# A two-block transformer kernel on one core: the joint before the second block's first site, with rows transposed before the final norm scales them

## The chip, the cores and the metric

One Trainium2 chip, one core of it. The time is the device time of one execution in microseconds, the median of three runs for the kernel before. TensorE does the matrix products, VectorE and ScalarE the elementwise work, GpSimd a few adds and some loads, SyncE issues the weight loads.

## The reference

The input is one sequence of 256 tokens with 1024 features. A first block of two layers (attention, convolution, Fourier and spatial gating branches, modulated by a conditioning vector) ends in a root-mean-square norm. A second block follows, two layers of three parts each, which the kernel calls sites 0 to 5: feed-forward, mixer, feed-forward, twice.

```
x, xc = layer 0, layer 1                      # first block
x = rmsnorm(x, final_g)                       # the final norm
for layer in range(2):                        # second block
    x = x + 0.5 * rmsnorm(swiglu(rmsnorm(x, g[0])), g[1])   # site 0 or 3
    x = x +       rmsnorm(mixer(rmsnorm(x, g[2])), g[3])    # site 1 or 4
    x = x + 0.5 * rmsnorm(swiglu(rmsnorm(x, g[4])), g[5])   # site 2 or 5
rmsnorm(x, g) = x * rsqrt(mean(x * x) + 1e-6) * g
```

All of it is float32. The products of the second block split each operand into a high part, rounded to the fast float32r format, and a low part, the remainder, and add three products: high by high, low by high, high by low.

## The kernel before

**Residual.** `X` holds the 256 tokens as two tiles t of 128 rows, each handled in two halves hf of 512 columns. At the end of layer 1 four output banks, one for each (t, hf), are multiplied by a gate row on VectorE (`out_scaled`, L1133, into two buffers `ytmp`, one for each hf) and added to `X`, by GpSimd (L619), or by VectorE for the pairs in `ADDED` (L1137). `x_half(L, t, hf)` names whichever add it is.

**The joint.** ScalarE takes the squares of `X` and the root of the final norm (L891 to L896), VectorE the reciprocal (L1368) and `final_scaled` (L1372), which multiplies `X` by it and by the gain `final_g`. TensorE then transposes `X` in chunks of 128 columns (`turned`, L2215) into banks, ahead of it `warm` filler products (L2206) that nobody reads. ScalarE makes the high part of chunk c out of the bank (`input_high`, L912), with the gain of site 0's norm as scale, VectorE the low part HL (`input_ready`, L1394). The root of site 0's own norm is not applied to the inputs: it is taken meanwhile (`x_square`, `inverse`), laid out as a row by two small products (`norm_sum`, L2232) and a copy (`norm_row`, L921), and multiplied into the gate sums behind the products (`gate_scaled`, L1446).

**A feed-forward site.** Hidden columns come in 22 chunks of 128. Units of 1024 columns of weights, numbered a, a+1, ... from `unit_base[i]`, go through a ring of three slots in SBUF (1 MB a slot, two units), each split by `high` on ScalarE (L879) and `low` on VectorE (L1361, its semaphore `s_low` counts the units) into six buffers. Units a to a+4 are gate, up, gate, up and down of the first pair; a+5 gate and a+6 up of the next pair, a+7 the second down row of the first. TensorE's order is gate_up(0), norm_sum, gate_up(1), down(0), and then a loop of gate_up(0), down(1), gate_up(1), down(0) per pair; L2254 and L2255 are the products of gate and up, L1765 those of down. VectorE sums the halves of a bank (`gate_parts` L1442, `up_parts` L1454), multiplies by the silu of the gate (L1459) and makes `hidden_low` (L1468); ScalarE does `silu` (L946) and `hidden_high` (L952). ScalarE's order in the first pair is silu(0), high(a+6), hidden_high(0), high(a+7). VectorE's is low(a+4), gate_scaled, low(a+5), multiplied, hidden_low(0), low(a+6).

**Queues.** Each engine works its own list in the order written. SyncE issues a weight load into a slot when the last low of the slot's two units is done (L498, in the loop L527): the gate slot of the second pair waits for low(a+2), the up slot for low(a+3), the down slot for low(a+7). In the joint VectorE does the lows of units 0 to 3 ahead of `out_scaled`. GpSimd issues the load of the gain row of site 0's second norm when `final_scaled(1, 1)` is done, and behind it that of `alibi`, a table of the mixer (L557).

## Time and profile before

| | |
|---|---|
| runs | 1490.28, 1492.75, 1494.66 us |
| median | 1492.75 us |
| profiled execution, its own time | 1492.96 us |
| its span, first to last instruction | 1491.2 us |
| busy in it | TensorE 1452.5 us (97%), VectorE 985.8 (66%), ScalarE 702.3 (47%), GpSimd 66.2 (4%) |
| mean granted TensorE clock | 0.996 |
| HBM traffic | 162 GB/s over the span |

The runs lie within 0.3% of each other. The time of the profiled execution is its span and 1.8 us around it. Times in the rows of a trace are microseconds from the start of the span. A busy share says how full an engine is, not where it stands still.

### The profile page before, as it was taken

What the parts mean: (1) busy time and instruction counts of PE and PEld (TensorE: products, weight loads), DVE (VectorE), ACT (ScalarE), POOL (GpSimd) and SP (SyncE); (2) the same over time, 40 slices, a digit from 0 to 9 for tenths busy, and PEclk for the clock granted to TensorE, in tenths of its full rate; (3) what the DMA queues carried; (4) which work ended last, traced back from release to release, by engine and by line L of the source; (5) the groups of instructions that cost most, each with busy time, mean ns of one, the idle gap of its engine ahead of it and who ended that gap; (6) DMA issues with size and microseconds to landing.
All of it is one profiled execution on the core that took longest, in us unless ns stands there. A gap on an engine that the chain in (4) does not pass through costs nothing.

```text
span 1491.2 us, 22138 instructions
## 1 busy us (share of the span) xinstructions
PE 1452.5 (97%) x8141; PEld 1174.5 (79%) x8141; DVE 985.8 (66%) x1631; ACT 702.3 (47%) x1212; POOL 66.2 (4%) x91
## 2 busy tenths in 40 slices
PE   5999999999999999999999999999999999999998
PEld 3778746877855888889888888878888888788887
DVE  2588335165345777777787777786777776877776
ACT  3433136141245444466566444464444756554444
POOL 0200120020101000000010000000000001000000
PEclk9999999999999999999999999999999999999999
DMA  9532166245316556646434566546566554455662
GB/s 331 196 91 79 57 194 219 85 132 170 112 57 208 170 178 205 208 156 170 142 114 156 169 198 200 193 159 193 169 197 199 178 145 143 127 167 171 195 197 88
DMA packets 197717, 242.96 MB, mean 163 GB/s; under 512 B 4464, under 2 KB 179088, under 8 KB 197520
## 3 DMA queue, kind: packets, MB, share of 16 engines
q1 hardware_dynamic: 194560, 229.43, 48.5%
q0 software_dynamic: 2512, 10.49, 2.0%
q10 hardware_dynamic: 576, 2.10, 0.4%
q8 instruction: 46, 0.75, 0.2%
q14 instruction: 23, 0.19, 0.0%
HBM read 240.95 MB, written 1.05 MB: 162 GB/s over the span
## 4 chain that ended last, share of the span: by engine, by line
PE 89%; DVE 4%; DMA 3%; ACT 2%; issue 1%; SPq 0%; POOL 0%; DVEq 0%; ACTq 0%; POOLq 0%
PE bank L1765 39%; PE bank L2254 20%; PE bank L2255 10%; PE bank L1884 5%; PE bank L2162 1%; PE bank L1743 1%; DMA weight_ring<-in_w_ada 1%; DVE input_split L1394 1%; DMA weight_ring<-in_w_ffn_up 1%; DVE weights_low L1361 1%; PE bank L2107 1%; PE bank L2070 1%; PE bank L2029 1%; ACT weights_high L879 1%; PE bank L2079 1%
## 5 line engine op out<-in xcount | busy, mean ns | idle before, releaser
L1361 DVE TENSOR_TENSOR weights_low<-weight_ring,weights_high 128x1024 fp32r<-128x1024 f32 x328 | 393.1, 1221 | 133.4 <-ACT weights_high L879 133.2
L2254 PE MATMUL bank<-input_split,weights_high 128*128 128x512 f32 x1344 | 479.2, 399 | 1.6 <-DVE input_split L1394 1.3
L879 ACT ACTIVATE weights_high<-weight_ring 128x1024 fp32r<-128x1024 f32 x328 | 334.9, 1048 | 105.3 <-PE bank L1765 62.0
L2255 PE MATMUL bank<-input_split,weights_low 128*128 128x256 f32 x1344 | 376.9, 280 | 0.0
L2254 PEld LDWEIGHTS bank<-input_split,weights_high 128*128 128x128 f32 x1344 | 252.4, 188 | 65.6 <-issue 2.2
L2255 PEld LDWEIGHTS bank<-input_split,weights_low 128*128 128x128 f32 x1344 | 253.7, 189 | 3.0
L1765 PE MATMUL bank<-weights_high,hidden_high 128*128 128x512 f32 x352 | 138.0, 392 | 0.3 <-DVE hidden_low L1468 0.3
L1765 PE MATMUL bank<-weights_low,hidden_high 128*128 128x512 f32 x352 | 137.9, 392 | 0.0
L1765 PE MATMUL bank<-weights_high,hidden_low 128*128 128x512 f32 x352 | 137.0, 389 | 0.0
L946 ACT ACTIVATE silu_gate<-gate_sum 128x256 f32<-128x256 f32 x88 | 36.8, 418 | 206.8 <-DVE gate_sum L1446 203.8
L1765 PE MATMUL bank<-input_split,weights_high 128*128 128x256 f32 x640 | 117.9, 286 | 1.4 <-DVE input_split L1394 1.3
L1765 PEld LDWEIGHTS bank<-input_split,weights_high 128*128 128x128 f32 x640 | 99.3, 191 | 3.5 <-issue 1.4
L952 ACT ACTIVATE hidden_high<-hidden 128x256 fp32r<-128x256 f32 x88 | 36.8, 418 | 128.2 <-DVE hidden L1459 126.7
L1765 PE MATMUL bank<-weights_high,input_split 128*128 128x256 f32 (+1 forms) x384 | 90.2, 323 | 0.5 <-issue 0.5
L1765 PE MATMUL bank<-input_split,weights_low 128*128 128x256 f32 x320 | 90.4, 283 | 0.0
L1765 PEld LDWEIGHTS bank<-weights_high,hidden_high 128*128 128x128 f32 x352 | 66.1, 188 | 15.7 <-issue 0.6
L1765 PEld LDWEIGHTS bank<-weights_high,hidden_low 128*128 128x128 f32 x352 | 66.1, 188 | 14.5
L1765 PEld LDWEIGHTS bank<-weights_low,hidden_high 128*128 128x128 f32 x352 | 66.1, 188 | 10.8
L1884 PE MATMUL bank<-hT,weight_ring 128*128 128x256 f32 (+1 forms) x304 | 73.5, 399 | 0.5 <-ACT hT L701 0.5
L1765 PEld LDWEIGHTS bank<-weights_high,input_split 128*128 128x128 f32 x384 | 64.4, 190 | 8.6 <-issue 3.5
L1884 PEld LDWEIGHTS bank<-hT,weight_ring 128*128 128x128 f32 x304 | 58.3, 194 | 13.3 <-issue 5.7
L1468 DVE TENSOR_TENSOR hidden_low<-hidden,hidden_high 128x256 fp32r<-128x256 f32 x88 | 37.4, 425 | 45.2 <-ACT hidden_high L952 45.2
(329 smaller groups left out, 2098.9 us busy)
## 6 DMA issues: line engine op xcount, KB each, us to landing
weight_ring<-in_w_ffn_gate SPq DMA_DIRECT2D x44, 1024.0 KB, 5.3
weight_ring<-in_w_ffn_up SPq DMA_DIRECT2D x44, 1024.0 KB, 5.3
weight_ring<-in_w_ffn_down SPq DMA_DIRECT2D x44, 1024.0 KB, 4.9
weight_ring<-in_w_in SPq DMA_DIRECT2D x32, 1024.0 KB, 5.3
weight_ring<-in_w_ada SPq DMA_DIRECT2D x24, 1024.0 KB, 6.8
weight_ring<-in_w_out SPq DMA_DIRECT2D x16, 1024.0 KB, 5.0
weight_ring<-in_w_in SPq DMA_DIRECT2D x24, 512.0 KB, 4.9
gain_row<-in_norm_gains POOLq DMA_DIRECT2D x6, 512.0 KB, 4.0
```

What stands on the lines that cost most here:

```text
L879: A(unit_in(WH, U), unit_source(U), ACT.Copy).then_inc(s_high, 1)
L946: A(sgate[:, par, :], gsum[:, par, :], ACT.Silu).then_inc(s_silu, 1)
L952: A(HBH[:, par if to is None else to, :], hbuf[:, par, :], ACT.Copy).then_inc(s_hh, 1)
L1361: TTn(unit_in(WL, U), unit_source(U), unit_in(WH, U).bitcast(F32), ALU.subtract).then_inc(s_low, 1)
L1394: STT(HL[:, c, :], B[X_BANK[c]][:, half * T:(half + 1) * T], vT[:, 2, R_PRE + 8 * i + c:R_PRE + 8 * i + c + 1], HH[:, c, :].bitcast(F32), ...
L1468: TTn(HBL[:, to, :], hbuf[:, par, :], HBH[:, to, :].bitcast(F32), ALU.subtract).then_inc(s_hl, 1)
L1743: last = mm(b[32 * (k % 4):32 * (k % 4) + 32, q * T:(q + 1) * T], CS[:, k, :], cols(n)[:, k, :], start=(k < 4), stop=(k >= 4), skip_group_ ...
L1765: last = mm(o, lhs(x), rhs(y), start=start and m == 0, stop=stop and m == 2, skip_group_check=True)
L1884: last = mm(b[out_rows, 0:ncol], lhs(k), hT[:, k, 0:ncol], start=(k == 0), stop=(k == KD - 1))
L2029: last = mm(b[:, sg * T:(sg + 1) * T], FA[:, 2 * sg + tl, m, cs * P:(cs + 1) * P], dft_n[:, cs, tl, :], start=(g == 0), stop=(g == 3))
L2254: mm(b[:, :].rearrange("p (h n) -> p h n", h=2), unit_in(WH, U)[:, k, :], HX[:, k, :, :], start=(k == 0), stop=False, skip_group_check=True)
L2255: last = mm(b[:, 0:T], unit_in(WL, U)[:, k, :], HH[:, k, :], start=False, stop=(k == KD - 1), skip_group_check=True)
```

## The change

The edits, all of them about the joint and site 0:

- `ADDED` for layer 1: VectorE adds (0, 1) too, so that GpSimd has two adds and VectorE two.
- VectorE does the lows of units 0 and 1 alone ahead of `out_scaled`; low(2) comes after the HLs of site 0, low(3) after `final_scaled(1)`.
- TensorE transposes `X` as it leaves layer 1, unscaled. `input_high` and HL multiply by `first_gain`, the product of final_g and site 0's gain, made at the start from a row added to the packed vectors.
- `final_scaled(t)` still scales `X` in place, as the residual needs it, but tile 0 after its transposes (`x_read`) and before the HLs, tile 1 after the HLs and low(2).
- The final root of tile 0 is taken as before; the last square and the root of tile 1, and the squares of site 0's norm, come after the eight input_high on ScalarE.
- `inverse(0)` also multiplies by the final norm's inverse root, and eps times the mean by the final root's square, in small operations on 128x2.
- For site 0 `norm_sum` moves from between gate_up(0) and gate_up(1) to the middle of gate_up(1), `gate_parts` behind `inverse`, and high(4) ahead of the root.
- Filler: one `warm` instead of six ahead of site 0's transposes, and one more between the tiles.
- GpSimd's two loads wait for `s_low` of 31 as well.

```diff
-ADDED = [{(0, 1), (1, 1)}, {(1, 1)}]
+ADDED = [{(0, 1), (1, 1)}, {(0, 1), (1, 1)}]
...
             pool.wait_ge(*at("final_scaled", 1, 1))
+            pool.wait_ge(s_low, unit_base[0] + 31)
             load(gain_row[:, :], I["norm_gains_2"][0, 1].partition_broadcast(P), "gain_loaded")
...
+            final_square(0, 0)
+            final_square(0, 1)
+            final_root(0)
+            final_square(1, 0)
...
             def site_norm(i):
-                for hf in range(2):
-                    x_square(i, 0, hf)
+                if i == 0:
+                    act.wait_ge(*at("first_gain"))
+                else:
+                    for hf in range(2):
+                        x_square(i, 0, hf)
...
+                if i == 0:
+                    final_square(1, 1)
+                    final_root(1)
+                    for hf in range(2):
+                        x_square(0, 0, hf)
                 for hf in range(2):
                     x_square(i, 1, hf)
+                if i == 0:
+                    high(unit_base[i] + 4)
...
+            TTn(first_gain[:, :], vT[:, 2, R_PRE:R_PRE + 8], vT[:, 2, R_FG:R_FG + 8], ALU.mult).then_inc(*done("first_gain"))
...
                 if L:
-                    for unit in range(EARLY):
+                    for unit in range(2):
                         low(unit)
...
+            def final_scaled(t):
                 dve.wait_ge(*at("final_root", t))
-                dve.reciprocal(stat[:, 12 + t:13 + t], stat[:, 8 + t:9 + t]).then_inc(*done("inverse", "final", t))
+                dve.reciprocal(stat[:, 56 + t:57 + t], stat[:, 54 + t:55 + t]).then_inc(*done("inverse", "final", t))
                 dve.wait_ge(*at("inverse", "final", t))
+                dve.wait_ge(*(at("x_T", "site", 0, 5) if t else at("x_read", 0)))
...
+            final_scaled(0)
...
+                if i == 0:
+                    low(2)
+                    final_scaled(1)
+                    low(3)
...
+                if i == 0:
+                    TTn(stat[:, 12:14], stat[:, 12:14], stat[:, 56:58], ALU.mult).then_inc(*done("inverse", "both"))
+                    dve.wait_ge(*at("inverse", "both"))
...
-                gate_parts(0, a + 1)
+                if i:
+                    gate_parts(0, a + 1)
                 inverse(i)
+                if i == 0:
+                    gate_parts(0, a + 1)
...
-                        pe.wait_ge(*(at("x_new", i - 1, t, c // 4) if i else at("final_scaled", t, c // 4)))
+                        pe.wait_ge(*(at("x_new", i - 1, t, c // 4) if i else x_half(1, t, c // 4)))
...
-                warm(1 if i else WARM)
+                warm(1)
                 turned(0, (0, 1, 2, 3))
                 warm(1)
                 turned(0, (4, 5, 6, 7))
+                if i == 0:
+                    warm(1)
                 turned(1, (0, 1, 2, 3, 4, 6, 5, 7))
...
                     for q in range(2):
+                        if between is not None and q:
+                            norm_sum(between)
...
-                norm_sum(i)
+                if i:
+                    norm_sum(i)
...
-                gate_up(1, a + 2, f0 if n else None)
+                gate_up(1, a + 2, f0 if n else None, between=None if i else 0)
```

## Rows read from the trace of the kernel before

**Rows 1.** The page, part 4: the chain that ended last, share by engine.

```profile
PE 89%; DVE 4%; DMA 3%; ACT 2%; issue 1%; SPq 0%; POOL 0%; DVEq 0%; ACTq 0%; POOLq 0%
```

**Rows 2.** Chain of waits in the joint: start, length, what.

```profile
476.02 2.06 DVE input_split L1394 x5
```

**Rows 3.** Timeline of TensorE: start, length, line, operation, tiles, shape, count, idle before.

```profile
459.99 7.10 PE L2162 MATMUL bank<-weight_ring,gated 128*128 128x512 f32 x16 [0.57 <-DVE gated L1309]
...
473.39 0.68 PE L2215 MATMUL bank<-const_base,residual 128*128 128x128 f32 x4 [1.15 <-DVE residual L1372]
...
488.83 0.39 PE L1765 MATMUL bank<-weights_high,hidden_high 128*128 128x512 f32 x1
...
513.99 0.40 PE L1765 MATMUL bank<-weights_high,hidden_high 128*128 128x512 f32 x1
...
581.08 0.40 PE L1765 MATMUL bank<-weights_high,hidden_high 128*128 128x512 f32 x1
```

**Rows 4.** Timeline of VectorE, the joint and site 0's loop.

```profile
463.86 3.50 DVE L1361 TENSOR_TENSOR weights_low<-weight_ring,weights_high 128x1024 fp32r<-128x1024 f32 x3 [2.09 <-ACT weights_high L879]
467.28 1.28 DVE L1133 TENSOR_TENSOR scaled_out<-bank,gate_rows 128x512 f32<-128x512 f32 x2
...
471.46 0.93 DVE L1137 TENSOR_TENSOR residual<-residual,scaled_out 128x512 f32<-128x512 f32 x1
...
474.09 1.41 DVE L1372 SCALAR_TENSOR_TENSOR residual<-residual,stat,gain_row 128x512 f32<-128x512 f32 x2
...
478.67 0.88 DVE L1394 SCALAR_TENSOR_TENSOR input_split<-bank,vectors_T,input_split 128x256 fp32r<-128x256 f32 x2 [0.21 <-ACT input_split L912]
...
512.36 0.43 DVE L1468 TENSOR_TENSOR hidden_low<-hidden,hidden_high 128x256 fp32r<-128x256 f32 x1 [0.48 <-ACT hidden_high L952]
...
553.95 2.36 DVE L1361 TENSOR_TENSOR weights_low<-weight_ring,weights_high 128x1024 fp32r<-128x1024 f32 x2 [0.53 <-ACT weights_high L879]
...
578.11 0.43 DVE L1468 TENSOR_TENSOR hidden_low<-hidden,hidden_high 128x256 fp32r<-128x256 f32 x1 [0.48 <-ACT hidden_high L952]
```

**Rows 5.** Timeline of ScalarE: the root, the inputs, the first pair.

```profile
471.39 0.29 ACT L896 ACTIVATE stat<-stat 128x1 f32<-128x1 f32 x1
...
475.51 2.30 ACT L912 ACTIVATE input_split<-bank,vectors_T 128x256 fp32r<-128x256 f32 x6 [0.43 <-PE bank L2215]
...
485.55 1.05 ACT L879 ACTIVATE weights_high<-weight_ring 128x1024 fp32r<-128x1024 f32 x1
486.82 0.42 ACT L952 ACTIVATE hidden_high<-hidden 128x256 fp32r<-128x256 f32 x1 [0.22 <-DVE hidden L1459]
```

**Rows 6.** Timelines of GpSimd and of SyncE: adds, and issues of loads.

```profile
468.11 3.73 POOL L619 TENSOR_TENSOR residual<-residual,scaled_out 128x512 f32<-128x512 f32 x3 [55.10 <-DVE scaled_out L1133]
...
476.36 0.54 POOL L557 DMA_DIRECT2D alibi<-in_k_alibi  x1
...
467.87 0.39 SPq L527 DMA_DIRECT2D weight_ring<-in_w_ffn_gate  x1
468.44 0.43 SPq L527 DMA_DIRECT2D weight_ring<-in_w_ffn_up  x1
...
563.86 0.37 SPq L527 DMA_DIRECT2D weight_ring<-in_w_ffn_up  x1
```

**Rows 7.** Loads, all and the two of 467.87 and 468.44: size, us to landing.

```profile
weight_ring<-in_w_ffn_up SPq DMA_DIRECT2D x44, 1024.0 KB, 5.3
...
alibi<-in_k_alibi POOLq DMA_DIRECT2D x1, 1920.0 KB, 8.8
...
weight_ring<-in_w_ffn_gate SPq DMA_DIRECT2D x1, 1024.0 KB, 7.3
...
weight_ring<-in_w_ffn_up SPq DMA_DIRECT2D x1, 1024.0 KB, 9.6
```

**Rows 8.** Stretches: length, busy by engine, granted clock, DMA share, GB/s.

```profile
471.00:473.40 2.40, 1.25 (x4) 0.23 (x2) 2.33 (x5) 2.15 (x8) 0.83 (x1) 1.00 1.05 380
...
480.00:482.00 2.00, 2.00 (x13) 1.77 (x12) 1.57 (x7) 0.94 (x4) 0.00 (x0) 1.00 1.02 430
```

More of the change, by code:

```diff
@@ L61 @@
 R_BADA, R_NORM, R_QN, R_KVN, R_CW, R_CB, R_CLG, R_CLB, R_BPW, R_BF, R_C = 0, 24, 32, 34, 35, 97, 99, 101, 103, 105, 107
-R_SUB, R_PRE = 0, 2
+R_SUB, R_PRE, R_FG = 0, 2, 50
 N_DIL, N_DIFF, N_SB = 6, 4, 6
@@ L227, in program @@
         stat = sb("stat", [P, 64])
+        first_gain = sb("first_gain", [P, KD])
         eps = sb("eps", [P, 4])
@@ L435, in step, with pre_gain @@
             return v if j is None else j * per + v
+        def pre_gain(i, c):
+            return vT[:, 2, R_PRE + 8 * i + c:R_PRE + 8 * i + c + 1] if i else first_gain[:, c:c + 1]
         def y_out(i, t, hf):
@@ L902, in site_norm @@
             def site_norm(i):
-                for hf in range(2):
-                    x_square(i, 0, hf)
+                if i == 0:
[3 more added lines that the diff above has]
+                        x_square(i, 0, hf)
                 if i and SITES[i - 1][0] == "ffn":
@@ L911, in site_norm @@
                     half = c // 6
-                    A(HH[:, c, :], B[X_BANK[c]][:, half * T:(half + 1) * T], ACT.Copy, scale=vT[:, 2, R_PRE + 8 * i + c:R_PRE + 8 * i + c + 1]).then_inc(*done("input_high", i, c))
+                    A(HH[:, c, :], B[X_BANK[c]][:, half * T:(half + 1) * T], ACT.Copy, scale=pre_gain(i, c)).then_inc(*done("input_high", i, c))
+                if i == 0:
[3 more added lines that the diff above has]
+                        x_square(0, 0, hf)
                 for hf in range(2):
                     x_square(i, 1, hf)
+                if i == 0:
+                    high(unit_base[i] + 4)
                 act.wait_ge(*at("x_mean", "ready", i))
                 A(stat[:, 8:10], stat[:, 6:8], ACT.Sqrt).then_inc(*done("rms_ready", "site", i))
-                high(unit_base[i] + 4)
+                if i:
+                    high(unit_base[i] + 4)
                 if SITES[i][0] == "ffn":
@@ L1406, in inverse @@
                     dve.wait_ge(*at("x_mean", "ready", i))
-                    TS(stat[:, 10:12], stat[:, 6:8], 4 * RMS_EPS, None, ALU.mult).then_inc(*done("eps_scaled", i))
+                    if i == 0:
+                        for q in range(2):
+                            if q:
+                                dve.wait_ge(*at("x_mean", "rescaled", 0))
+                            TTn(stat[:, 10:12], stat[:, 10:12] if q else stat[:, 6:8], stat[:, 54:56], ALU.mult).then_inc(*done("x_mean", "rescaled", q))
+                        dve.wait_ge(*at("x_mean", "rescaled", 1))
+                    TS(stat[:, 10:12], stat[:, 6:8] if i else stat[:, 10:12], 4 * RMS_EPS, None, ALU.mult).then_inc(*done("eps_scaled", i))
                 dve.wait_ge(*at("rms_ready", "site", i))
@@ L2217, in turned @@
                             last.then_inc(*done("x_T", "site", i, c if c < 4 else c - 2))
+                        if i == 0 and t == 0 and c == 7:
+                            last.then_inc(*done("x_read", 0))
                 for r in hand_over(0):
                     pe.wait_ge(*at(*r))
-                warm(1 if i else WARM)
+                warm(1)
                 turned(0, (0, 1, 2, 3))
@@ L2224, in site_norm @@
                 turned(0, (4, 5, 6, 7))
+                if i == 0:
+                    warm(1)
                 turned(1, (0, 1, 2, 3, 4, 6, 5, 7))
@@ L2259, in ffn, with gate_up @@
                 f0 = n * FFN_CHUNKS
-                def gate_up(par, U, free, j=None, site=None):
+                def gate_up(par, U, free, j=None, site=None, between=None):
                     if free is not None:
@@ L2537 @@
     rows += [a["norm_gains_2"][l, 2 * q].reshape(-1, 128) for l in range(2) for q in range(3)]
-    rows.append(_np.zeros((128 - 50, 128), _np.float32))
+    rows.append(a["final_g"].reshape(-1, 128))
+    rows.append(_np.zeros((128 - 58, 128), _np.float32))
     arrays["k_vec2"] = _np.concatenate(rows)
```

25 lines of the change are left out of this document (13 added, 12 removed).

## The prediction

> **What bounds the kernel now.** I read the page first: TensorE holds 89% of the chain that ended last [rows 1], at a granted clock of 0.996 on average. Only a stretch in which TensorE stands or does filler can give time back. Of these the diff touches one, the joint between the second layer of the first block and site 0, so I read next the chain of waits there, then the timeline of each engine, then the DMA answers, and at last the steady loop of site 0, since two loads move into it.
>
> In this stretch the chain goes through VectorE's splits (low(1) to low(3)), two GpSimd adds, the scaling of the residual, the transposes and, from 476.02, the splitting of the inputs [rows 2]. The rows of TensorE [rows 3] say what this costs: the last output product ends at 467.09, then come six `warm` fillers and an idle 1.15 us, and transposes from 473.39. The products of site 0 follow the split inputs, and once the last of these is there TensorE runs without a wait: the down product of the first pair starts at 488.83.
>
> **The joint after the change.** I lay the new order out with the durations of before.
> VectorE: low(0) and low(1) alone stand ahead of out_scaled. The three lows of [rows 4] take 3.50, so each costs 1.14 start to start and 1.22 by itself, and low(1) ends at 463.86 + 1.22 = 465.1. Output (0,0) is final at about 464.5 (the 16 records of [rows 3] are eight products of 0.86; four of them close the four outputs). So out_scaled(0,0) and (0,1) run 465.0 to 466.3 instead of 467.28 to 468.56 [rows 4]: 2.3 earlier. VectorE then adds (0,1) itself, 0.93 by its present add beside GpSimd's [rows 4], to 467.3. GpSimd adds (0,0) in 1.24 (three take 3.73, [rows 6]), to 467.05. out_scaled(1,0) 467.3 to 467.95, GpSimd's (1,0) to 469.3; out_scaled(1,1) to 468.6 and VectorE's add to 469.5. The residual of tile 1 is complete at 469.5; before it was 472.4.
> TensorE: one filler, two records of 0.43 like those of the output, to 467.8, four transposes (0.68 the four in [rows 3]), filler 0.86, four more from about 469.1, filler, and tile 1 from about 470.4. Its first chunk is there at 470.55, against 475.51 before, where ScalarE starts the eight input_high [rows 5]. The scaling left the path of tile 1: 2 x 1.41 on VectorE [rows 4].
> ScalarE and VectorE meanwhile: from the first residual half (GpSimd's first add, 468.11 + 1.24) to the end of the root at 471.68 it took 2.3 [rows 5, 6], and from 467.05 the same ends at 469.35; final_scaled(0), 1.41 with a reciprocal ahead, waits for `x_read` (469.6) and ends at 471.05. The first HL waits for its input_high, 471.15. So the transposes and the scaling of tile 0 end together, and HL starts at 471.15 instead of 476.02: **4.9 us earlier**. If the order slips by a filler (0.86) it is 4.0; if both of VectorE's adds take 0.7 and not 0.93, and nothing else holds, it is 5.3. The small operations (`first_gain` at the start, where VectorE stands idle after the copy of the vectors; two more products and one more multiplication of 128x2, under 0.25 each by the reciprocal's share of that stretch, an estimate) are hidden: norm_diag is wanted only after unit a+2. The norm_sum is moved, not added.
>
> **What comes late instead.** Three things stand now between the HL of chunk 7 and TensorE's down product.
> VectorE: the last HL ends 479.55 - 4.87 = 474.7 [rows 4]; low(2) to 475.8; reciprocal and final_scaled(1) to 477.35; low(3) to 478.5; inverse with its extra products to 480.5 (norm_diag, wanted by TensorE at 480.7: no stall); gate_parts and up_parts to 481.75; low(a+4) from 481.7, where it ran some 1.9 later before. VectorE gains only 1.9 where TensorE gained 4.9.
> SyncE: the loads of the next pair's gate and up slots wait for low(2) and low(3). They were issued at 467.87 and 468.44 [rows 6]; now at 476.0 and 478.7. A load lands 5.3 after its issue in the median [rows 7], and with the tail of gate ahead of it I take 5.5, so up lands at 484.2. In ScalarE's order high(a+6), which reads it, stands ahead of hidden_high(0) (485.55 and 486.82, [rows 5]): high(a+6) to 485.2, hidden_high(0) to 485.6, hidden_low(0) to 486.05.
> TensorE wants to start down(0) at 488.83 - 4.87 = 483.96. It starts at 486.05: **2.1 us given back**. Without the late load it would still be 485.8 less 483.96 = 1.8, by VectorE's own queue; with the loads sharing (7.3 for gate, 0.8 behind a load, [rows 7]) up lands at 486.0 and it is 3.9. Those are the bounds, and I take 2.1 since the two issues lie 2.7 apart and a transfer by itself takes 2.9 (gate and up landed at 475.2 and 478.0, 2.9 apart, [rows 6, 7]).
> So TensorE is 2.8 early when it enters the loop, and VectorE 1.65. The tightest place of the loop's first pairs is down(1) at 513.99, with hidden_low(1) finished at 512.79 [rows 3, 4]: slack 1.2, of which 1.1 is now used. No stall, but nothing left there. Later pairs have more: at 581.08 against 578.54 it is 2.5 [rows 3, 4], and 1.4 after the change.
>
> **The two GpSimd loads.** gain_row (512 KB) and alibi (1920 KB, landing 8.8 later, [rows 7]) were issued in a row, alibi at 476.36 [rows 6], when SyncE's ring was nearly through and nothing waited for them. They now wait for the 31st low. Counting units, that is the first of the two at 553.95 [rows 4], so T = 555.2 on the clock of before. SyncE issues a down load behind the next low, about T + 1.2, then gate, and up at 563.86 [rows 6], T + 8.7. In this loop the up load is on VectorE's own cycle: landing, high, two lows, gate sum, silu, low, product, hidden_high, hidden_low(1), next issue. That cycle takes 16.4 us (512.36 to 578.11 are four) and TensorE's 16.77 (513.99 to 581.08), [rows 3, 4], so TensorE waits only when an up load is later than the slack.
> GpSimd's bytes are 2.49 MB. At the ring's rate (2.9 us for 1.05 MB) they take 6.8 us. Of the 11.8 us from T + 2.3 to the normal landing of up at T + 14.1 (5.4 behind its issue), the three ring loads use 8.6, and 3.2 lie idle. So up lands 3.6 late. At the 430 GB/s of the stretch in which GpSimd's loads ran nearly alone [rows 8] they take 5.8, and it is 2.6. Less the slack of 1.4, TensorE stalls 2.2 or 1.2 at the down(1) near 581. Below that the price is nothing, if the cover is larger than I count; above, 5.4, if no idle time absorbs anything (6.8 less 1.4). I take **2.0**, near the upper, because the ring's packets are in the mix all the time. The stall comes once: the cycle of VectorE then again runs faster than TensorE's.
> A rule that bears on this: the Trainium skill, DMA: Bandwidth & Descriptors, section Where 436 GB/s comes from, has the HBM of one core stop at about 358 GB/s and the fabric at 435. Ring loads ran at 1.05 MB in 2.9, some 362 GB/s, and one stretch of [rows 8] shows 430, above the first figure. By 358 alone the stall would be 2.3 and by 435 1.1, an estimate from that page; the row decides, and either lies within 0.1 of one of the two figures above.
>
> **Sum.** -4.9 + 2.1 + 2.0 = -0.8 us. The profiled execution took 1492.96 (span 1491.2 and 1.76 around it), which is 0.2 over the median of 1492.75. So 1492.2 on that scale and **1492.0** as a median.
>
> **Rivals.**
> *The loads are covered.* If the loop's slack or the DMA's idle time takes the two loads, only the first give-back stands: -2.8, 1490.0. For it: 2.5 us of slack before; against it: the up load is on the cycle. 0.24.
> *Nothing is given back.* If hidden_low(0) is in time and the loads are covered, all of the joint stays: -4.9 to -5.3, 1487.7. VectorE's queue speaks against it, since low(2), low(3) and final_scaled(1), 1.14 + 1.41 + 1.22, are moved behind the inputs. 0.10.
> *The joint doesn't get shorter.* If final_scaled(0), which now stands between the adds and the HLs on VectorE, waits for an `x_read` that comes behind bank hand-overs, VectorE becomes the bound. Late by two fillers and four transposes (2 x 0.86 + 0.68 = 2.4), the joint gives -2.5; VectorE is late as well, so both prices stay: +1.6, 1494.4. 0.06.
> *Slower: the loads in mid-site cost more than the joint gives.* GpSimd's packets go first and the ring waits for all of it, 6.8 late, less 1.4 of slack: 5.4 with -2.8 gives +2.6, 1495.4; it decides above a lateness of 4.2. If VectorE's cycle, once late, then also misses the next ring slot, the price comes twice and passes +4.5. 0.10, of which 0.03 over 0.3%.
> *Slower: TensorE's clock falls.* Four fillers go on balance and a stand of 2.1 comes at down(0). At half clock the 32 product pairs of the first four units, 0.35 each, would cost 11 more: +10, 1503. The row of 471 to 473.4, 1.25 us busy in 2.4, still shows 1.00 [rows 8]. 0.03.
>
> **How the numbers follow.** The forecast has 0.47 (its own range 1490.8 to 1493.2). The cases above hold 0.53. A difference of 0.3% is 4.5 us, about what a measurement of this kernel can tell from none. Only "nothing given back" passes it downward, and not surely; with an overall error of the joint's size I give 0.10 to faster, 0.05 to slower, 0.85 to no change. The range leaves out the clock case and the ends: 1488.2 to 1495.2.
>
> **What would show it.** The first transposes near 467.8 and the first HL near 471.2 show the joint; final_scaled(1) before low(3) and the gate and up issues near 476 and 479 show the move; an idle 2 us ahead of the first hidden_high product of site 0, released by hidden_low(0), shows the give-back; the alibi issue near 554 and an idle TensorE ahead of the down product near 578 to 580, with high waiting for up before it, the mid-site price. Wrong would be: no idle at down(0); the up load landing in time; or an idle at every pair of the loop.

## The result, and the profile after

The changed kernel takes 1496.74 us (median of 20 runs, 1493.11 to 1502.66) and the kernel before 1491.73 (20 runs, 1489.13 to 1494.66): 1.0036 times as long, 95% interval 1.0027 to 1.0046. It is slower by 5 us. 1492.0 was forecast, and 1496.74 lies above the range's end of 1495.2. One later execution of the changed kernel took 2902.58 us, which nothing on record explains; no ratio below counts it.

The profiled execution of the changed kernel has a span of 1497.6. Its last output product ends at 470.74 and not at 467.09, most of it because TensorE's granted clock was 0.82, 0.50 and 0.66 in the three stretches of 5 us from 30 to 45 us, long before the changed code (in the kernel before it was 1.00 there). So I compare by the distance to the first filler behind the output products, 466.93 before and 470.57 after, and call it the joint's start. This is TensorE's timeline of after in the joint: start, length, line, operation, tiles, shape, count, idle before.

```profile
470.57 1.02 PE L2250 MATMUL bank<-const_base 128*128 128x512 f32 x2
471.43 0.60 PE L2259 MATMUL bank<-const_base,residual 128*128 128x128 f32 x4
...
474.02 1.04 PE L2259 MATMUL bank<-const_base,residual 128*128 128x128 f32 x8
476.06 0.47 PE L2302 MATMUL bank<-input_split,weights_high 128*128 128x512 f32 x1 [1.01 <-DVE input_split L1422]
...
490.62 0.77 PE L1809 MATMUL bank<-weights_high,hidden_high 128*128 128x512 f32 x1 [2.07 <-DVE hidden_low L1509]
...
577.29 0.49 PE L1809 MATMUL bank<-weights_high,hidden_high 128*128 128x512 f32 x1 [1.11 <-DVE hidden_low L1509]
...
587.17 0.49 PE L1809 MATMUL bank<-weights_high,hidden_high 128*128 128x512 f32 x1 [1.23 <-DVE hidden_low L1509]
```

The joint is what was meant: transposes at once, one filler (two records) between groups, the first product of site 0 at 476.06. VectorE's timeline answers to [rows 4]:

```profile
470.17 1.33 DVE L1161 TENSOR_TENSOR residual<-residual,scaled_out 128x512 f32<-128x512 f32 x1
471.43 1.27 DVE L1157 TENSOR_TENSOR scaled_out<-bank,gate_rows 128x512 f32<-128x512 f32 x2
472.74 1.26 DVE L1161 TENSOR_TENSOR residual<-residual,scaled_out 128x512 f32<-128x512 f32 x1
...
474.11 1.41 DVE L1398 SCALAR_TENSOR_TENSOR residual<-residual,stat,gain_row 128x512 f32<-128x512 f32 x2
475.44 2.43 DVE L1422 SCALAR_TENSOR_TENSOR input_split<-bank,first_gain,input_split 128x256 fp32r<-128x256 f32 x6
...
478.88 1.22 DVE L1385 TENSOR_TENSOR weights_low<-weight_ring,weights_high 128x1024 fp32r<-128x1024 f32 x1
...
489.94 0.43 DVE L1509 TENSOR_TENSOR hidden_low<-hidden,hidden_high 128x256 fp32r<-128x256 f32 x1 [1.25 <-ACT hidden_high L974]
```

The first HL comes 4.87 behind the joint's start (475.44 less 470.57) where before it came 9.09 behind (476.02 less 466.93): 4.22 earlier. At the first down product the idle 2.07 stands, released by hidden_low(0). And here is ScalarE, which answers to [rows 5], and the stretch of the down product (windows: length, busy of PE, PEld, DVE, ACT, POOL, granted clock, DMA share, GB/s):

```profile
488.55 1.06 ACT L884 ACTIVATE weights_high<-weight_ring 128x1024 fp32r<-128x1024 f32 x1 [0.97 <-PE bank L2303]
489.51 0.40 ACT L974 ACTIVATE hidden_high<-hidden 128x256 fp32r<-128x256 f32 x1
...
571.73 1.06 ACT L884 ACTIVATE weights_high<-weight_ring 128x1024 fp32r<-128x1024 f32 x1 [5.33 <-DMA weight_ring<-in_w_ffn_down]
```

```profile
490.00:495.00 5.00, 4.38 (x12) 3.54 (x13) 4.69 (x7) 1.48 (x3) 0.00 (x0) 0.66 0.05 6
495.00:500.00 5.00, 5.00 (x30) 4.37 (x29) 2.79 (x3) 3.02 (x4) 0.00 (x0) 1.00 0.83 248
```

The granted clock, 1.00 up to 490, is 0.66 in the five us from there: 2.4 GHz fell to 1.2 for a time. The twelve records of the down product take 4.39 from the first to the next product, where they took 2.74 before. The issues of SyncE and GpSimd in mid-site answer to [rows 6], and the landings to [rows 7]:

```profile
559.48 0.57 POOL L561 DMA_DIRECT2D gain_row<-in_norm_gains  x1 [86.03 <-DVE weights_low L1385]
560.05 0.54 POOL L561 DMA_DIRECT2D alibi<-in_k_alibi  x1
```

```profile
560.25 0.37 SPq L531 DMA_DIRECT2D weight_ring<-in_w_ffn_down  x1
...
567.69 0.37 SPq L531 DMA_DIRECT2D weight_ring<-in_w_ffn_up  x1
581.37 0.37 SPq L531 DMA_DIRECT2D weight_ring<-in_w_ffn_down  x1
```

```profile
alibi<-in_k_alibi POOLq DMA_DIRECT2D x1, 1920.0 KB, 10.3
weight_ring<-in_w_ffn_gate SPq DMA_DIRECT2D x1, 1024.0 KB, 10.5
weight_ring<-in_w_ffn_up SPq DMA_DIRECT2D x1, 1024.0 KB, 9.8
```

A ring load that lands 5.3 after its issue in the median takes 9.8 to 10.5 here, and the down load issued at 560.25, right behind the two, takes 11.5 and holds ScalarE for 5.33 up to 571.73.

This table gives the down products of site 0, which has 22 of them, as distances from the joint's start, in us. "After, second profile" is the changed kernel in a later run (label after_again), in which the clock did not fall.

| | before | after | after, second profile |
|---|---|---|---|
| first HL | 9.09 | 4.87 | 4.64 |
| first down product | 21.90 | 20.05 | 19.73 |
| second | 30.28 | 29.99 | 28.17 |
| fourth | 47.06 | 46.75 | 46.01 |
| tenth | 97.38 | 97.07 | 96.43 |
| eleventh | 105.77 | 106.72 | 106.36 |
| thirteenth | 122.54 | 125.10 | 124.71 |
| twentieth | 187.01 | 189.57 | 189.17 |
| first product of site 1 | 199.89 | 203.05 | 203.86 |

From the first product of site 1 to the end it is 824.3 before, 824.0 and 823.8 after, and 823.5 to 825.5 in all profiles. So the changed kernel loses 3.2 to 4.0 in this stretch. It gains 4.2 to 4.5 at the inputs, has 0.3 to 1.0 of it left at the tenth down product, and loses 2.9 to 3.1 in mid-site and 0.6 to 1.8 at the site's end.

Outside of the span lie 2.20 us, where before 1.84 (means of the runs). That 0.36 came with every kernel that has the new joint, and I did not find what makes it.

The runs differ by stretches of half clock at different places, mostly in the first 50 us and around 200. Below I therefore also give a span "at equal clock". It corrects each run's span by 1.20 us for each 0.001 of its mean granted clock (fitted within the kernels over 296 runs, an estimate). It is rough, since the clock is told to 0.001 and a fall beside a wait costs less; I read no difference below 1 from it. By it before has 1485.9 and after 1489.1 (116 and 31 runs).

### The profile page after: what moved, and what is told of

Same layout as the page of the kernel before. It is cut to its first block, busy times and chain, and to the rows that moved or that the text cites. A ratio compares the mean times of both kernels' runs of the same rounds, so it can differ in the third digit from the quotient of the medians.

```text
span 1497.6 us, 22132 instructions
## 1 busy us (share of the span) xinstructions
PE 1455.5 (97%) x8133; PEld 1176.3 (79%) x8133; DVE 987.4 (66%) x1636; ACT 702.3 (47%) x1212; POOL 64.9 (4%) x90
## 4 chain that ended last, share of the span: by engine, by line
PE 90%; DVE 3%; DMA 3%; ACT 2%; issue 1%; SPq 0%; POOL 0%; DVEq 0%; ACTq 0%
PE bank L1809 39%; PE bank L2302 20%; PE bank L2303 10%; PE bank L1928 5%; PE bank L2206 2%; DMA weight_ring<-in_w_ada 2%; PE bank L1787 1%; DVE input_split L1422 1%; PE bank L2151 1%; DMA weight_ring<-in_w_ffn_down 1%; PE bank L2114 1%; PE bank L2073 1%; PE bank L2176 1%; PE bank L1803 1%; PE bank L2123 1%
```

## The experiments

Each has 10 to 12 runs (loads_at_joint and hidden_first 6, lows_ahead 8), taken beside the kernel before on the same chip (medians of before 1491.62, 1491.53, 1491.91 and 1492.04 in the four lots). A number in brackets behind a ratio is its 95% interval. "Entry" is the first product of site 1 from the joint's start, against 199.89 before.

**Loads at the joint.** After without GpSimd's wait for the 31st low.

```diff
             pool.wait_ge(*at("final_scaled", 1, 1))
-            pool.wait_ge(s_low, unit_base[0] + 31)
             load(gain_row[:, :], ...
```

> The changed kernel with GpSimd's two loads issued right behind final_scaled(1,1), as in the kernel before. Theory A (the mid-site loads are what makes the change slower: 2.9 us in its trace): the two stands of TensorE in the loop near 577 and 587 vanish, and the time falls by about 2.9 against the changed kernel, unless the loads now meet the late gate and up loads of the joint. Rival B (they only move): the up load of the second pair shares the DMA engines with 2.49 MB, lands 3 to 6 us later, and the stand ahead of down(0), 2.1 us in the changed kernel, grows to 5 to 8; the time is then equal to the changed kernel's or 1 to 4 us above it, some 5 to 9 above before.

1499.38 us, 1.0051 (1.0031 to 1.0070). No stand in mid-site, but one at the first down product, TensorE's timeline and the windows around it:

```profile
499.24 0.76 PE L1808 MATMUL bank<-weights_high,hidden_high 128*128 128x512 f32 x1 [9.39 <-DVE hidden_low L1508]
```

```profile
495.00:499.00 4.00, 0.00 (x0) 0.00 (x0) 0.44 (x2) 1.84 (x3) 0.00 (x0) 0.50 0.14 49
499.00:504.00 5.00, 4.76 (x12) 3.84 (x13) 4.45 (x7) 1.49 (x4) 0.00 (x0) 0.55 0.13 14
```

The up load of the second pair, issued 0.3 behind alibi, lands 13.1 later, and ScalarE waits 8.30 for it: entry 207.47. Rival B had the mechanism, and the stand is longer than its 5 to 8. The wait for the 31st low is thus no mistake in itself; it trades 7.6 for 3.2.

**Lows ahead.** After with low(2) and low(3) ahead of out_scaled again.

```diff
-                    for unit in range(2):
+                    for unit in range(EARLY):
                         low(unit)
...
                 if i == 0:
-                    low(2)
                     final_scaled(1)
-                    low(3)
```

> The changed kernel with low(2) and low(3) back ahead of out_scaled, so that the gate and up loads of the second pair are issued near 468 as before. Theory A (the stand at down(0) and the clock that falls in it come from the moved lows): the joint gives 2.3 less than in the changed kernel (1.9 to 2.6 against before instead of 4.2), but no stand ahead of down(0), no half-clock stretch near 490, and against the changed kernel the time falls by 1.0 to 2.5. The mid-site price stays at 1 to 3. In all 0 to 2 us over before. Rival B (the stand comes from VectorE's own queue): the stand stays at over 1 us and nothing is won.

1496.98 us, 1.0038 (1.0023 to 1.0053). First HL at 7.01, so the two lows were worth 2.1 of the joint's 4.2. The stand at the first down product is 1.29, the clock stays, and the time does not fall against the changed kernel, as theory A had it. Entry is 205.24, the worst but one: in this profile the up load of the third pair, issued 29.38 behind the joint's start and so no earlier than before, lands only at 38.75 (36.53 before), and TensorE stands at the fourth down product though a lead of 0.41 alone arrives there:

```profile
513.48 0.49 PE L1807 MATMUL bank<-weights_high,hidden_high 128*128 128x512 f32 x1 [1.67 <-DVE hidden_low L1507]
```

What made that load late is not shown.

**Fillers ahead of the first down product.** After with four more.

```diff
+                if i == 0:
+                    pe.wait_ge(s_up, 1)
+                    for _ in range(4):
+                        mm(B[0][:, :], ident, KB[:, 0:512], start=True, stop=True)
                 down(0, a + 4, f0 + 1, True)
```

> The changed kernel with four filler products of 512 columns on TensorE between gate_up(1) and down(0) of site 0, behind a wait that has long been met, so that TensorE is busy for 1.7 of the 2.1 us in which it stood. Theory A (the stand made the clock fall): granted clock 1.00 near 490 to 495, the twelve records of down(0) take 2.75 and not 4.4, down(0) itself starts when it did; the time falls by 1.5 against the changed kernel in the median. Rival B (the clock fell there by chance or for what went before): some runs still show it and the median moves by less than 0.5.

1495.61 us, 1.0035 (1.0020 to 1.0051). TensorE has no stand there, the granted clock is 1.00 in 480 to 490, and the second down product is at 29.38. Entry 202.48. The ratio is that of the changed kernel (1.0036), so a gain of 1.5 by keeping the clock up is not there.

**Before, with only the loads moved.**

```diff
             pool.wait_ge(*at("final_scaled", 1, 1))
+            pool.wait_ge(s_low, unit_base[0] + 31)
             load(gain_row[:, :], ...
```

> The kernel before with one line of the change alone: GpSimd's two loads also wait for the 31st low. Theory A (the loads cost by themselves): the slack of 2.5 at down(1) near 581 is overrun by the up or down load that comes late by 3 to 5, and the time rises by 1.0 to 2.0. Rival B (they cost only since the change had used up the slack): rise of 0 to 0.5.

1495.09 us, 1.0025 (1.0011 to 1.0038). The waits of TensorE in site 0 (engine, tile, line, releaser: total, times, longest), where the kernel before has none:

```profile
PE bank L1766 <- DVE hidden_low L1469: 1.9, 3, 1.1
```

The down products equal before up to the tenth (within 0.12), then come 2.1 later by the thirteenth, and the entry is 203.11: 3.2 later. At the site's end ScalarE waits 1.52 for a down load, at 650.77, a wait that before doesn't have. By the medians this part of the change alone costs 3.5 of the 5.0, more than either theory had.

**alibi early.** After with the load of alibi ahead of GpSimd's residual additions; gain_row stays in mid-site.

```diff
+                if L:
+                    pool.wait_ge(*at("attn", 1, 0, 1))
+                    load(alibi[...], I["k_alibi"], "alibi_loaded")
                 for t in range(nq // P):
...
-            pool.wait_ge(*at("attn", 1, 0, 1))
-            load(alibi[...], I["k_alibi"], "alibi_loaded")
```

> The changed kernel with the 1.92 MB load of alibi issued by GpSimd ahead of its residual additions at the end of the first block (about 450 us, where the DMA queues are half idle); gain_row (0.5 MB) stays in mid-site. Theory (the transfer of alibi in mid-site makes a down load and an up load late, TensorE stands twice, and at the site's end VectorE and ScalarE have lost their lead): the two mid-site stands (2.3 together in the changed kernel) vanish or fall below 0.6, the site 1 entry comes at +199.4 to +200.3 after the joint's start instead of +203.05 (before: +199.89), the median is 2.5 to 3.5 below the changed kernel: ratio to before 1.0010 to 1.0020, what is left being the clock behind the joint and the outside of the span. Rival (any GpSimd load in mid-site, however small, costs the stand, since ScalarE is blocked in its order): at least 1.5 us of stands stay, ratio 1.0030.

1494.34 us, 1.0017 (1.0001 to 1.0033), the ratio as expected. From the tenth to the thirteenth down product it loses 0.5 and not 2.9. But the entry is 201.54, where 199.4 to 200.3 was expected: at the site's end ScalarE waits 1.68 for a down load, and a stand of 0.68 on hidden_low and 0.7 at the next joint follow. So even 0.5 MB in mid-site seem to take ScalarE's and VectorE's lead.

**hidden_high first.** After, order alone.

```diff
-                high(a + 6)
+                if i:
+                    high(a + 6)
                 hidden_high(0, f0 + 1, None)
+                if i == 0:
+                    high(a + 6)
```

> The changed kernel with ScalarE's hidden_high(0) ahead of high(a+6) in the first pair of site 0, order alone. Theory (the stand of 2.07 at the first down product is the late up load, behind which hidden_high waits): the stand falls to 1.0 to 1.5, VectorE's own queue setting it; the clock behind it may stay at its upper level; median 0.5 to 2 us below the changed kernel, 1.0025 to 1.0033. Rival (VectorE's queue alone makes the stand): it stays at 1.9 to 2.1 and the ratio at 1.0036.

1497.90 us, 1.0048 (1.0029 to 1.0067). The stand fell to 1.30, as the theory has it, the clock stayed, and the second down product came 2.56 ahead of before. The time did not fall. TensorE's timeline at the fourth down product:

```profile
513.75 0.49 PE L1812 MATMUL bank<-weights_high,hidden_high 128*128 128x512 f32 x1 [1.38 <-DVE hidden_low L1512]
```

The lead falls there from 2.56 to 1.02. That is a second place of giving back, and my expectation, which stopped at the first, missed it. Mid-site takes 4.1 here (first stand 2.37); over the seven profiles of the changed joint with both loads in mid-site it takes 2.7 to 4.1.

**Combined.** After with alibi early, hidden_high first and two fillers.

> The changed kernel with alibi loaded early, hidden_high(0) first, and two fillers (1.7 us) ahead of the first down product. Theory: first HL 4.2 early, down(0) about 2.5 early, clock 1.00 behind it, no stand in mid-site, site 1 entry at +197.3 to +198.5; median 1489.5 to 1491.5, ratio 0.9985 to 1.0000. Rival (the lead can't be kept, since VectorE's cycle in the first pairs gives it back wherever it is longer than 1.2): site 1 entry at +199.5 or later and ratio 1.0005 or more.

1494.57 us, 1.0023 (1.0006 to 1.0039); entry 199.74, down products ahead by 2.96, 2.56, 2.56 and then 1.12. The rival held: leads above about 1 are lost at the fourth down product. The time was still 3 above before while site 1 was entered no later, so some of the loss lay outside of what I had looked at.

**Before with the early product.** Before with the eight rows of final_g, the tile `first_gain` and the product that writes it, which nothing reads.

```diff
+        first_gain = sb("first_gain", [P, KD])
         eps = sb("eps", [P, 4])
...
+            TTn(first_gain[:, :], vT[:, 2, R_PRE:R_PRE + 8], vT[:, 2, R_FG:R_FG + 8], ALU.mult)
```

> The kernel before with only the early part of the change: eight more rows of final_g in the vectors and the one VectorE product that makes first_gain, which nothing reads here. Theory (it is hidden behind the vectors' copy): ratio 0.9995 to 1.0005, the joint starts where it does in before. Rival (it delays the start, or the different start sets other clock stretches in the first 50 us): the joint's start 1 to 4 us later, ratio 1.0007 or more.

1493.98 us, 1.0014 (1.0000 to 1.0028), entry 200.07. The interval touches 1; at equal clock the span is 1488.1 against 1485.9. Something in "one small product, hidden" seems to cost.

**Before with the tile alone.** No instruction, no data.

```diff
+        unused = sb("unused", [P, KD])
         eps = sb("eps", [P, 4])
```

> The kernel before with one unused tile of 8 floats a partition allocated where the change allocates first_gain, and nothing else: no instruction, no data. Theory (the tile moves all that is allocated behind it by 32 bytes, and the products of the first block that read first_high and hT then take 1 to 1.5% longer, spread over 44 to 300 us): ratio 1.0008 to 1.0018, the joint's start 1.3 to 2.4 us later at equal clock, the product of first_high by hT_low at 359 ns and not 354. Rival (the instruction that writes first_gain, or its data, makes the 2 us): ratio 0.9995 to 1.0005 and 354 ns.

1490.72 us, 1.0001 (0.9987 to 1.0014): the ratio missed what I expected. At equal clock it is 1487.7 against 1485.9, and the trace shows longer products in the first block. Groups of TensorE in 60 to 300 us, this kernel (busy us, mean ns of one):

```profile
L1766 PE MATMUL bank<-hT_high,first_high 128*128 128x512 f32 x126 | 52.1, 413 | 0.0
L1766 PE MATMUL bank<-hT_low,first_high 128*128 128x512 f32 x127 | 50.3, 396 | 0.0
L1766 PE MATMUL bank<-first_high,gated_low 128*128 128x512 f32 x61 | 24.0, 394 | 0.0
```

and the kernel before:

```profile
L1765 PE MATMUL bank<-hT_high,first_high 128*128 128x512 f32 x123 | 50.3, 409 | 0.0
L1765 PE MATMUL bank<-hT_low,first_high 128*128 128x512 f32 x124 | 48.8, 393 | 0.0
L1765 PE MATMUL bank<-first_high,gated_low 128*128 128x512 f32 x61 | 23.7, 389 | 0.0
```

The group that the expectation names, first_high by hT_low, has 359 and 354 as foretold, but it is no measure: it mixes two shapes and lies between 351 and 359 in the other profiles with the tile.

**The gain in place.** After, with the product written over the rows of final_g in `vectors_T`, and no tile.

```diff
-        first_gain = sb("first_gain", [P, KD])
...
-            TTn(first_gain[:, :], vT[...], vT[...], ALU.mult)
+            TTn(vT[:, 2, R_FG:R_FG + 8], vT[...], vT[...], ALU.mult)
```

> The changed kernel without the tile first_gain: the product is written over the eight rows of final_g in vectors_T, so that all other tiles lie where they lay before. Theory (the tile's place costs 1.5 to 2.1 of the changed kernel's 5): median 1494.3 to 1495.3, ratio 1.0018 to 1.0026. Rival (the place costs nothing): 1.0033 to 1.0040.

1495.04 us, 1.0020 (1.0006 to 1.0033). In its profile the stand at the first down product is 2.42, the clock stays at 1.00, and the lead of 1.9 falls to 0.2 at the fourth (idle 1.55); entry 204.17.

**A tile of 64 bytes.** After, with `first_gain` of 16 floats, of which the product fills the first 8.

```diff
-        first_gain = sb("first_gain", [P, KD])
+        first_gain = sb("first_gain", [P, 2 * KD])
```

> The changed kernel with first_gain of 16 floats a partition and not 8, so that what is allocated behind it moves by 64 bytes and not 32. Theory (what costs is the place within 64 bytes): as gain_in_place, ratio 1.0018 to 1.0026, and 354 ns for the product of first_high by hT_low. Rival (any move costs): ratio 1.0033 to 1.0040 and 359 ns.

1495.16 us, 1.0027 (1.0011 to 1.0043). Groups of TensorE in the same stretch, of this kernel:

```profile
L1809 PE MATMUL bank<-hT_high,first_high 128*128 128x512 f32 x128 | 52.1, 407 | 0.0
L1809 PE MATMUL bank<-hT_low,first_high 128*128 128x512 f32 x128 | 50.6, 396 | 0.0
L1809 PE MATMUL bank<-first_high,gated_low 128*128 128x512 f32 x50 | 19.6, 392 | 0.0
```

The product of hT_high by first_high has a mean of 413 or 414 ns in all nine kernels with the 32-byte tile, 409 or 410 in all that lack it, and 407 here. But hT_low by first_high has 396 here, as with the 32-byte tile (395 or 396) and not as without one (393 or 394), and first_high by gated_low lies between the two. So that a shift by 64 bytes costs nothing is not shown; its ratio lies between those of gain_in_place and after, within the noise of both.

**Best.** After with the gain in place, both GpSimd loads at the end of the first block (the gain row of site 0 in softplus's tile, which is free by then), hidden_high first and two fillers.

```diff
+                    load(ZP[:, :, :].rearrange("p a b -> p (a b)")[:, 0:D], I["norm_gains_2"][0, 1]..., "gain_loaded")
```

> The changed kernel with four things: first_gain in place; both GpSimd loads at the end of the first block (the gain row of site 0 in a tile of its own, in the place of softplus); hidden_high(0) ahead of high(a+6); two fillers ahead of the first down product. Theory (VectorE's cycle in the first two pairs lets TensorE keep about 1.0 of the joint's gain, nothing is lost in mid-site, and the lead at the site's end is kept): site 1's entry 0.3 to 1.0 ahead of before, ratio 0.9990 to 1.0003. Rival (a lead of TensorE without one of VectorE and ScalarE is lost at the site's end whatever the loads do): entry at -0.3 to +0.3, ratio 1.0000 to 1.0006.

1488.58 us, 0.9985 (0.9969 to 1.0000). TensorE's timeline at the fourth down product:

```profile
509.14 0.49 PE L1810 MATMUL bank<-weights_high,hidden_high 128*128 128x512 f32 x1 [2.27 <-DVE hidden_low L1510]
```

The lead is 2.51 up to the third down product and 0.09 from here; the entry is 199.92, as before's, which is the rival's, while the ratio is below both expectations. Nothing is lost in mid-site or at the site's end.

Three more, on one chip, for what was open. **After again**, unchanged:

> The changed kernel once more, as the measure of the other two on one chip. All theories: ratio 1.0027 to 1.0046, median about 5 above before; two stands of about 1.2 in mid-site; at down(0) a stand of about 2, after which either the clock falls and the lead on before is 0.3 at the second down product, or it doesn't, and the lead of 1.9 is given back at the fourth down product.

1495.92 us, 1.0034 (1.0022 to 1.0046); its profile stands in the table above. **Best again**, unchanged:

> The kernel of best once more. Theory (its 3.3 below before are real): ratio 0.9975 to 0.9992, median 1488.0 to 1490.0. Rival (they were a fortunate draw of the clock's stretches; the trace of site 0 shows 0.0 against before): ratio 0.9995 to 1.0005.

1490.08 us, 0.9990 (0.9980 to 1.0001), entry 199.14, lead at the fourth down product 0.84. **Before with the loads early**: the loads of best, and nothing else of it.

> The kernel before with both GpSimd loads moved from behind the joint to the end of the first block (the gain row of site 0 in a tile of its own), and nothing of the joint changed. Theory A (what best gains comes from the loads being out of the way of the first ring loads of site 0, the up load of the second pair landing earlier): ratio 0.9980 to 0.9992, its site 1 entry ahead of before by 0.2 or more. Theory B (those loads were covered in before, and best gains by the joint): ratio 0.9996 to 1.0004, entry within 0.2 of before.

1490.63 us, 0.9991 (0.9980 to 1.0002), entry 200.01. Its entry is that of theory B and its ratio that of theory A; neither is shown. Over both lots best has a mean of 1490.12 (23 runs) and before of 1492.11 (62 runs), 2.0 us less (interval 0.9 to 3.0), but by the times best can't be told from before with the loads early: 1490.12 and 1490.61 (12 runs). At equal clock their spans are 1484.4 and 1485.6, of which 0.36 comes back outside of the span. So the version that beats both kernels is there, by 0.13%; a share of the joint in it is hinted at and not shown.

## Why the prediction was wrong

The joint and the first down product came out near the forecast. What failed is the sentence "No stall, but nothing left there" on the fourth down product, the price of 2.0 for the loads in mid-site with "The stall comes once", and `first_gain`, which was costed at nothing.

**The joint, -4.9 forecast.** The mechanism held, the size was 4.2 to 4.5. VectorE's additions took 1.33 and 1.26, not the 0.93 of [rows 4]. That put final_scaled(0) at 3.54 behind the joint's start, and the HLs, not the transposes, were last: TensorE idles 1.01 ahead of its first product. Two lows moved behind the inputs are worth half of it (lows_ahead).

**The give-back at down(0), 2.1.** It held. The stand is 1.96 to 2.42 in five profiles of the changed joint, 1.30 with hidden_high first and 1.29 with the lows ahead. So the late split of the up unit makes some 0.7 and VectorE's queue the rest. The forecast said 1.8 without it; here it was less. In after the profile puts the start of the split high(a+6), 17.98 behind the joint's start, down to a product (idle 0.97), but the load landed at 17.96 as well; in gain_in_place the split waited for the load (1.17).

**The step that failed first: "No stall, but nothing left there".** The prediction had TensorE enter the loop 2.8 early and VectorE 1.65, and found 1.2 of slack at the fourth down product, of which 1.1 would be used. The runs show a stand there in all six profiles in which a lead of about 2 arrives, 0.90 to 2.27 us long, after which 0.1 to 1.1 of the lead is left. What sets the start there is the third pair's up load, whose split stands ahead of the silu and hidden_high of this product in ScalarE's order. These are the splits that wait for it, in the kernel before:

```profile
503.56 2.01 ACT L879 ACTIVATE weights_high<-weight_ring 128x1024 fp32r<-128x1024 f32 x2 [1.34 <-DMA weight_ring<-in_w_ffn_up]
```

and in the changed kernel's second profile, with the idle of the product behind it:

```profile
501.21 2.01 ACT L884 ACTIVATE weights_high<-weight_ring 128x1024 fp32r<-128x1024 f32 x2 [1.73 <-DMA weight_ring<-in_w_ffn_up]
```

```profile
510.84 0.49 PE L1809 MATMUL bank<-weights_high,hidden_high 128*128 128x512 f32 x1 [0.90 <-DVE hidden_low L1509]
```

That is 36.63 and 36.38 behind the joint's start. TensorE was 2.1 ahead, the load was issued 1.3 earlier (27.69 against 28.98), and its data came 0.25 earlier, since this load and the down and gate loads ahead of it are issued within 5 us and move at 343 to 384 GB/s once gate has started. In all seven profiles with a stand there, lows_ahead's included, the product starts 9.62 or 9.63 behind the start of that split; in the kernel before it starts 10.43 behind, so there was 0.8 to spare. I took VectorE's lead from its own queue and forgot that the loads stand on this path. The landing itself lies between 35.5 and 37.3 in all profiles but those of lows_ahead (38.75) and loads_at_joint, and what is left of a lead goes with it: best keeps 0.09 and best again 0.85, with landings at 37.25 and 36.48. With that, the joint's change could bring about 1 us, whatever became of down(0).

**The clock, a rival at 0.03.** In after the granted clock fell behind the stand at down(0), and the twelve records took 1.65 longer. The rival had a fall through the products of the first four units and 10 us. It came later, at the place I had named as its cause, and was short. It did not come in every execution: of the profiled kernels with a stand there it fell behind stands of 2.07, 2.19, 2.24 and 9.39 and did not behind 1.29, 1.30, 1.96 and 2.42. It hardly mattered, for the lead that it takes is taken at the fourth down product otherwise: after keeps 0.31 and its second profile 0.95.

**The mid-site loads, +2.0.** Mis-sized: 2.9 in after, 3.1 in its second profile, and 3.2 with the site's end in the kernel before with this part alone, in which no slack had been used. The bytes were not wrong: the two loads and the ring's three share the queues at up to 467 GB/s, as the DMA view of 559 to 582 in after has it (40 equal slices):

```profile
GB/s 0 0 0 121 342 192 351 248 378 467 420 353 419 467 420 379 452 306 385 403 374 383 386 349 349 346 356 345 345 322 139 5 0 0 0 0 0 0 0 0
```

The 358 GB/s of the Trainium skill (DMA: Bandwidth & Descriptors, Where 436 GB/s comes from) is passed by many slices, as in [rows 8], and a few lie above its 435 as well; over the 8.6 us from 563.6 it is 399, over the 15.5 us from 561.3 it is 359. It decided nothing. Three things were wrong. The down load is the one that lands late first (issued 0.2 behind alibi; ScalarE has it 11.5 later). VectorE waits 5.16 for the split of it and, working in order, makes the gate sum only behind that, so that silu starts at 575.23 and hidden_low at 576.74. Then a second stand of 1.23 follows ten us behind the first: "The stall comes once" is false. No load is waited for ahead of it. The steps of VectorE's cycle are uneven: in the kernel before hidden_low comes 10.46 behind the one of 567.65 and the next 6.00 behind that, and here it comes 9.87 behind the first stand's, where TensorE wants it after about 8.6. And the lead of ScalarE and VectorE over TensorE is not won back in the seven down products that follow: at the site's end ScalarE waits 1.40 for a down load, at 659.26, and the next joint pays 0.6 to 1.8 once more.

These are the lines of VectorE in after, and below them one of the kernel before:

```profile
572.83 1.23 DVE L1385 TENSOR_TENSOR weights_low<-weight_ring,weights_high 128x1024 fp32r<-128x1024 f32 x1 [5.16 <-ACT weights_high L884]
...
576.74 0.42 DVE L1509 TENSOR_TENSOR hidden_low<-hidden,hidden_high 128x256 fp32r<-128x256 f32 x1 [0.56 <-ACT hidden_high L974]
...
586.61 0.43 DVE L1509 TENSOR_TENSOR hidden_low<-hidden,hidden_high 128x256 fp32r<-128x256 f32 x1 [0.48 <-ACT hidden_high L974]
```

```profile
567.65 0.43 DVE L1468 TENSOR_TENSOR hidden_low<-hidden,hidden_high 128x256 fp32r<-128x256 f32 x1 [0.56 <-ACT hidden_high L952]
```

The slower rival ("the loads in mid-site cost more than the joint gives", 0.10) gave the nearest time, 1495.4, by luck: it has one late ring load, a stall of 5.4 and 2.8 of the joint left, and the runs show two stands of 1.1 to 1.4 and a lead that was gone before.

**The edit costed at nothing: `first_gain`.** The product is hidden, as forecast (0.17 at 11.34 us, VectorE idle behind it for 2.73). Its tile isn't free. It lies ahead of hT, first_high and the rest, and moves them by 32 bytes. The distance from the first product of hT_high to the joint's start is 423.4, 423.7 and 424.5 with it (filler_down, before_tile_only, after_again) and 421.9 to 422.1 in five profiles without it, all with a granted clock of 1.00 in that stretch: 1.3 to 2.6 us. With the time at half clock counted half, an estimate, the other profiles fall into the same two groups, 423.1 to 425.3 with the tile and 421.7 for the kernel before; tile_64, at 423.5, falls in with the first. At equal clock the spans of the two kernels that only add the tile are 2.0 above before (24 runs against 116, interval 1.6 to 2.4). By medians alone it is not shown (1.0014 and 1.0001).

**The sum.** At the entry of site 1 the forecast had -0.8, and the two profiles have +3.2 and +4.0. Of the difference the joint makes 0.7 and 0.4, the first down product 0.3 and 0.2, what is lost from there to the tenth 1.5 and 1.2 (forecast 0; behind down(0) by the clock in the first profile, at the fourth down product in the second), mid-site 0.9 and 1.1, and the site's end 0.6 and 1.8 (forecast 0). The entry gives 3.2 to 4.0, the tile 1.3 to 2.6, the outside of the span 0.36: 4.9 to 7.0, and 5.0 was measured. At equal clock the spans differ by 3.2 alone, less than these terms add up to; the correction takes off the falls beside a wait as well, so it may count too little here. I can't divide it further.

## What to carry to other kernels

When a joint gets shorter, follow the engine that gains into the loop until the first wait for a transfer of the loop's own, and take that transfer's landing, not the engine's, as what sets the time there: here a gain of 4.2 to 4.5 us was 1.9 to 2.2 behind the first product, and behind the fourth 0.3 to 1.0 was left. A load on another queue costs by the first ring load behind it and by what the waiting engines, which work in order, can't do meanwhile; put it where the queues are idle and no one waits for the loads behind it. And allocate a small new tile behind the large ones, or inside one that has room, and compare the mean time of the untouched products.

## What the runs showed of the hardware

Moving TensorE's fp32r operands by 32 bytes a partition made a 128x512 product take 413 or 414 ns and not 409 or 410 on average, and the first block 1.3 to 2.6 us longer; what a move by 64 bytes does is open (407 in one group, 396 and not 393 in another). With 2.5 MB of GpSimd's loads beside them, ring loads of 1 MB landed 9.8 to 11.5 after their issue and not 5.3. And the same stand of about 2 us was followed by a fall of the granted clock in one execution of the changed kernel and by none in another.
